# Two ScalarE copies and a small square root change places in the attention loop of a two-block fp32 network

## The reference

```
q, k, v = jnp.split(qkv, 3, axis=-1)          # 8 heads, each with 2 x 64 query/key rows and 128 value rows
...
s = jnp.where(dist >= 0, s + bias, -jnp.inf)
p = jax.nn.softmax(s, axis=-1)
a = (p[:, :, 0] - lam * p[:, :, 1]).astype(v.dtype)
outs.append(jnp.einsum('bhqk,bkhe->bqhe', a, v[:, :qe]))
...
o = _rmsnorm(o, subln_g) * (1.0 - lam_init)
return jnp.einsum('ble,ed->bld', o.reshape(bsz, L, N_HEADS * V_DIM), w_out)
```

## Time and profile before

| | |
|---|---|
| median of 3 runs | 1658.22 us (1657.4 to 1659.14) |
| profiled execution, its own time | 1659.31 us |
| its span, first to last instruction | 1657.5 us |
| TensorE (PE) busy | 1571.1 us, 95% |
| VectorE (DVE) busy | 786.5 us, 47% |
| ScalarE (ACT) busy | 620.3 us, 37% |
| GpSimd (POOL) busy | 529.9 us, 32% |
| granted TensorE clock, mean over the span | 0.985 of full speed |

### The profile page before, as it was taken

The page is one execution under the profiler, slowest core; times in us unless marked ns, Lnnn a source line. Parts: engine busy times, 40 slices in busy tenths (PEclk is TensorE's granted clock), DMA queues, the critical chain, the costliest instruction groups (busy, mean ns, idle before and its releaser), DMA issues.

```text
span 1657.5 us, 31409 instructions
## 1 busy us (share of the span) xinstructions
PE 1571.1 (95%) x12656; PEld 1408.2 (85%) x12656; DVE 786.5 (47%) x1368; ACT 620.3 (37%) x1135; POOL 529.9 (32%) x235
## 2 busy tenths in 40 slices
PE   7999997999999999999999999999999989999895
PEld 6888886999999999989989888888889867777764
DVE  4333433654232231574445642332316799556655
ACT  5556665443222231332224432232324434433321
POOL 3122222134444444124431344444441244450020
PEclk9999999999999999999999999999999999999998
DMA  5121111222233322222222223232322122200001
GB/s 181 52 60 56 52 52 39 90 76 91 89 90 97 95 90 90 77 77 90 89 88 77 77 91 100 89 102 89 101 90 77 63 79 87 89 16 3 3 26 51
DMA packets 35401, 125.66 MB, mean 76 GB/s; under 512 B 3920, under 2 KB 4048, under 8 KB 35280
## 3 DMA queue, kind: packets, MB, share of 16 engines
q1 hardware_dynamic: 35280, 123.90, 23.5%
HBM read 121.79 MB, written 2.10 MB: 75 GB/s over the span
## 4 chain that ended last, share of the span: by engine, by line
PE 69%; DVE 11%; issue 2%; ACT 2%; DMA 0%; DVEq 0%; ACTq 0%; SPq 0%
PE G L1415 58%; PE G L1685 3%; PE ST L1685 3%; PE PV L1685 1%; PE ST L1388 1%; PE PO L1685 1%; DVE rstd L863 1%; DVE acc L1319 1%; DVE wlo L902 1%; DVE t L1169 0%; DVE z L1172 0%; DVE m L922 0%; DVE z L1161 0%; ACT rms L535 0%; PE PO L1415 0%
## 5 line engine op out<-in xcount | busy, mean ns | idle before, releaser
L462 POOL TENSOR_TENSOR wlo<-raw,whi 128x1024 fp32r<-128x1024 f32 x209 | 506.6, 2425 | 1085.0 <-ACT whi L511 645.9
L1415 PE MATMUL G<-xh,whi 128*128 128x258 f32 (+3 forms) x1504 | 372.8, 310 | 11.7 <-DVE t L1008 6.9
L1415 PE MATMUL G<-xl,whi 128*128 128x258 f32 (+3 forms) x1504 | 358.9, 301 | 0.0
L1415 PE MATMUL G<-xh,wlo 128*128 128x258 f32 (+3 forms) x1504 | 356.9, 300 | 0.0
L1415 PE MATMUL G<-ah,whi 128*128 128x256 f32 (+2 forms) x1024 | 279.3, 314 | 4.7 <-DVE al L1144 2.9
L1415 PE MATMUL G<-al,whi 128*128 128x256 f32 (+2 forms) x1024 | 277.6, 312 | 0.0
L1415 PE MATMUL G<-ah,wlo 128*128 128x256 f32 (+2 forms) x1024 | 277.4, 312 | 0.0
L521 ACT ACTIVATE whi<-raw 128x1024 fp32r<-128x1024 f32 x112 | 118.7, 1060 | 417.3 <-PE G L1415 411.6
L1415 PEld LDWEIGHTS G<-xh,whi 128*128 128x128 f32 x1504 | 245.0, 190 | 30.4 <-issue 11.5
L1415 PEld LDWEIGHTS G<-xl,whi 128*128 128x128 f32 x1504 | 244.8, 190 | 10.5
L1415 PEld LDWEIGHTS G<-xh,wlo 128*128 128x128 f32 x1504 | 245.2, 190 | 9.4
(11 more groups left out here) (306 smaller groups left out, 2027.6 us busy)
## 6 DMA issues: line engine op xcount, KB each, us to landing
raw<-weights_dram SPq DMA_DIRECT2D x225, 512.0 KB, 3.6
hres<-xT_dram SPq DMA_DIRECT2D x8, 264.0 KB, 5.8
out_dram<-hres SPq DMA_DIRECT2D x8, 256.0 KB, 2.1
con<-consts_dram SPq DMA_DIRECT2D x1, 512.0 KB, 7.6
mat<-mats_dram SPq DMA_DIRECT2D x1, 512.0 KB, 8.4
con<-consts_dram SPq DMA_DIRECT2D x1, 392.0 KB, 5.3
vec<-vecs_dram SPq DMA_DIRECT2D x1, 203.0 KB, 2.6
```

The lines of the kernel that those rows point to most:

```text
L462: nc.gpsimd.tensor_tensor(wlo[:, s], raw[:, s % 2], whi[:, s].bitcast(F32), ALU.subtract)\
L1415: last_of[0] = nc.tensor.matmul(to[:, p0:p1], wt[:, w, ws], xt[:, k, t0 - off:t1_ - off], start=k == 0 and q == 0, stop=k == KT - 1 and q ...
```

## The change

The five lines that take the root of a finished head's norms are put into a function `head_root`. It is called in the turns with s % 3 == 0 behind the two copies into `vtok`, for the head before (seven calls, s = 6, 9, ..., 24, heads 0 to 6), and once behind the loop for head 7. Before, the same lines ended the body of the turns s = 5, 8, ..., 26.

```diff
+            def head_root(h):
+
+                act.wait_ge(oss_ready, 5 * (h + 1))
+                hs = slice(5 * h, 5 * h + 5)
+                nc.scalar.activation(orms[:, hs], oss[:, hs], ACT.Sqrt, scale=1.0 / P, bias=eps_t[:, 0:1])\
+                    .then_inc(orms_ready, 1)
+
             for s in range(TURNS):
                 prev, cur = tiles(s - 1), tiles(s)
                 if cur and s % 3 == 0:
...
                         .then_inc(v_copied, 1)
                     nc.scalar.activation(vtok[0:META, h % 2, 0, :], G[1][0:META, 0:P], ACT.Copy).then_inc(v_copied, 1)
+                    if h >= 1:
+                        head_root(h - 1)
                 if s % 3 == 1 and turned_head(s) is not None:
                     head_high(turned_head(s))
...
-                if prev and prev[-1] % 5 == 4:
-                    h = prev[-1] // 5
-                    act.wait_ge(oss_ready, 5 * (h + 1))
-                    hs = slice(5 * h, 5 * h + 5)
-                    nc.scalar.activation(orms[:, hs], oss[:, hs], ACT.Sqrt, scale=1.0 / P, bias=eps_t[:, 0:1])\
-                        .then_inc(orms_ready, 1)
+            head_root(HEADS - 1)
             head_high(HEADS - 1)
```

## The result

The changed kernel took 1647.11 us (median of 4 runs) against 1657.81 us of the kernel before, timed beside it: the ratio is 0.994, with a 95% interval of 0.9926 to 0.9954, so 7.6 to 12.3 us less. The forecast was 1649.5 us. The profiled execution took 1647.33 us, with a span of 1645.5 us.

The account below looks back on a forecast made before the run. TensorE, busy 1571.1 of 1657.5 us, was taken to bound the kernel. Six gains of 1.24 us plus 1.27, 8.7 in all at no added cost, from the median 1658.22 gave 1649.5 us, range about 1647 to 1653.2.

Parts of the forecast that it names:

- missing releaser: At the score matmul (L1528), TensorE's unnamed 8.2 us of waits end with ScalarE's second copy of the turned values.
- 1.24 us at six places and 1.27 at the last: Scores start earlier by these amounts at the seven places once the copies precede load and root; 8.7 us in all.
- control in turn 3: A turn without a root ahead of the copies: scores start 0.33 us after the last pair's start, no idle time.
- copies are early by 0.29 us: Turn 6: after the swap TensorE may go from 70.32, ahead of the scores' 70.61, so the gap closes wholly.
- sign of the copies within 0.05 us of that end: Expected in the new profile: at the seven places the copies start within 0.05 us of the sum of squares' end.
- rival of late copies: Something unseen holds copies or scores past 70.61 at the places; half the gain goes, 1653.8 us; chance 0.09.
- Cost of the moved pair: Table load and root behind the copies add 0 us, hidden in ScalarE's idle time before L658, cover 2.2 us.
- slower rival: Between second copy and L658, load and root collide with the exponentials above 5.0 us; at 5.5, 1661.7 us; chance 0.02.
- Nothing else comes late: In the attention loop TensorE sets the pace; ScalarE, VectorE, GpSimd and the weight stream move along, so the gain lasts.
- rival in which the gain is given back: Weight stream or ScalarE sets the loop's pace; only the last place's 1.27 us stays, 1656.9 us; chance 0.06.
- better-clock rival: TensorE's clock does not fall behind turn 24; PV to six pairs behind saves 1.6 us more, 1647.9 us; chance 0.15.

Follow-up runs that it names:

- e2: The changed kernel with the new order for heads 0, 1 and 2 alone, against the kernel before: 1653.75 us, ratio 0.9979.
- e4: The changed kernel with four scratch copies of 128x128 ahead of the copies of the turned values: 1655.36 us, ratio 0.9990 to the kernel before.
- e3: The changed kernel with one scratch copy of 128x128 ahead of the copies of the turned values: 1647.49 us, ratio 0.9949 to the kernel before.
- e5: The changed kernel with six scratch copies between the copies of the turned values and `head_root`: 1649.35 us, ratio 0.9955 to the kernel before.
- e6: The changed kernel with fourteen scratch copies between the copies of the turned values and `head_root`: 1664.3 us, ratio 1.0052 to the kernel before.
- e7: The changed kernel with `head_root` moved behind the first `turned_weights` (L658), ahead of the exponentials: 1659.42 us, ratio 1.0020 to the kernel before.
- e1: The changed kernel again with no edit, against the kernel before: 1648.69 against 1657.85 us, ratio 0.9949.

## Why the prediction was right

The forecast, faster by 8.7 us, held. In three comparisons the changed kernel was 10.0, 8.5 and 8.8 us faster by its ratios.

- *The missing releaser is the second copy.* Shown: the gap goes with it, stays where it is not early (e2), and comes back when something else delays it (e4).
- *1.24 us at six places and 1.27 at the last, 8.7 in all.* 8.53 measured, 1.22 a place. The control in turn 3 was the right yardstick: 0.33 us from the last pair to the scores there, and 0.33 at each changed place that is shown.
- *The copies are early by 0.29 us.* It was 0.39. The reckoning let the first copy start where the table load had started, behind the end of the sum of squares. It starts 0.10 us ahead of that end (68.61 against 68.52 plus 0.19). e3 shows that there is room, e4 that it is about this much. The sign of the copies within 0.05 us of that end was missed by this, on the good side. The rival of late copies rested on this margin and did not happen.
- *Cost of the moved pair: 0, under 2.2 us of cover.* The cover was 2.30 us, and 1.77 in turn 24. e5 used 1.9 of it at each place, all there was in turn 24, without loss. The reckoning for the first place was taken for all seven; in turn 24 TensorE comes to the turned weights sooner, and that cover was never worked out.
- *The slower rival decides above 5.0 us for the pair.* e6 puts it on the chip: scratch copies and pair take 6.3 us, and the period is 1.0 us longer than before. By this the point is near 5.3 us (an estimate: 6.3 less 1.0); but the rival left out the tail, where 3.1 us more are lost.
- *Nothing else comes late.* All periods behind the first are equal to 0.1 us, and no new wait appeared. The rival in which the gain is given back fell with that.
- *The clock.* The gap in turn 24 went, and the clock fell all the same, only later and for a shorter time: it was 1.00 in 244 to 248 and 0.57 in 248 to 252, against 0.54 and 0.61 in 254 to 258 and 258 to 262 before. What this spared lay ahead of PV, where TensorE has to wait for ScalarE anyway (the 0.47 us above). PV to six pairs behind took 4.28 us (248.41 to 252.69), against 4.27 in the earlier trace rows, so the better-clock rival brought nothing. In the first profile, what came on top of the 8.5 us was the earlier start of the loop and the clock in stages that the change does not touch. That the same put the first median 2.4 us below the forecast is likely and not shown, as only the profiled execution can be read by stages.

## What to carry to other kernels

A wait that the trace puts down to "issue" can be read from the order of time: look for the instruction whose end stands a fixed small distance ahead of the start, and for a place in the same trace where that instruction comes early. When a producer's copy stands behind upkeep with a table load, it is enough to swap them, if the idle time behind has room for the upkeep; that idle time must be read at every place, since here the last of seven had a quarter less. Past the cover the price can be more than the overrun, as in the tail of e7, where a longer wait of TensorE was followed by work at the lower clock. What moves in such a change is best measured as a distance between two starts inside the stage: for one program those agreed to 0.2 us from profile to profile (208.80 to 208.98 us), where the time of the whole kernel scattered by several.

## What had not been expected of the hardware

The scatter of this kernel is larger than the first runs told. The prediction took 1.7 us from three runs. Twenty-five executions of the kernel before, timed beside e1 to e4, lay between 1653.63 and 1661.15 us, and the mean granted clock went with them: 0.988 in the fastest, 0.983 in the slowest. 0.005 of 1657 us is 8.3 us, about the 7.5 us between the two; the executions in between follow the clock roughly, not strictly.

A table load starts behind the end of the instruction ahead of it (69.36 in turn 6 of the changed kernel, against 69.34), a plain copy in the same position up to 0.10 us ahead of that end. All loads in all profiles took 1283 ns, and the next instruction started 1.29 to 1.30 us behind the load's start wherever it had nothing else to wait for.
